# Another order of the transfers ahead of the second feed-forward product, and norm's sum, root and reciprocal at other places

## What is computed

```python
n2 = _rmsnorm(h, g_mlp[i])
h = h + jnp.square(jax.nn.relu(n2 @ w_ff1[i])) @ w_ff2[i]
n3 = _rmsnorm(h, g_ple[i])
h = h + jax.nn.sigmoid(n3 @ w_ple_gate[i]) * (p[i] @ w_ple[i])
```

## Time and profile before

| What | Value |
|---|---|
| Median of the runs | 1781.89 us (1781.26 to 1783.09) |
| The profiled execution, its own time | 1784.99 us |
| Span of its trace | 1782.2 us |
| PE busy | 1689.2 us, 95% of the span |
| DVE, ACT, POOL busy | 966.0, 624.0, 437.5 us |
| Mean DMA rate | 82 GB/s |
| PE, first feed-forward matmuls (line 2172) | about 177 + 175 + 175 us |
| PE, second feed-forward matmuls (line 1827, `wf_hi`, `wf_lo`) | about 159 + 159 + 159 us |

### The profile page before, as it was taken

How to read it: one execution, slowest core, us unless ns; L and a number is a source line. 1 busy time by engine, 2 the same in 40 slices (tenths; PEclk the granted TensorE clock), 3 DMA queues, 4 the chain that set the end, 5 groups by cost and what they waited for, 6 DMA issues and landing times.

```text
span 1782.2 us, 21830 instructions
## 1 busy us (share of the span) xinstructions
PE 1689.2 (95%) x8536; PEld 1325.1 (74%) x8536; DVE 966.0 (54%) x1489; ACT 624.0 (35%) x979; POOL 437.5 (25%) x250
## 2 busy tenths in 40 slices
PE   5899989999899999999999899999979999999997
PEld 4658778787656666668888688888858888888886
DVE  7359999960345566654345644444424444445424
ACT  5332332222355566721234334344412111113323
POOL 2212342222200000212214445445311222222220
PEclk8999999999999999999999999999989999999999
DMA  4202022243200020004432242332352222231112
GB/s 151 80 24 59 25 72 98 68 128 88 60 1 1 2 72 1 1 1 142 161 123 94 74 139 95 105 132 95 142 212 95 95 95 95 95 107 42 42 59 95
DMA packets 101742, 145.38 MB, mean 82 GB/s; under 512 B 17073, under 2 KB 83633, under 8 KB 101649
## 3 DMA queue, kind: packets, MB, share of 16 engines
q1 hardware_dynamic: 97808, 130.45, 22.5%
q10 hardware_dynamic: 3680, 13.63, 2.0%
q0 software_dynamic: 160, 0.02, 0.0%
HBM read 107.51 MB, written 34.73 MB: 80 GB/s over the span
## 4 chain that ended last, share of the span: by engine, by line
PE 86%; DVE 4%; issue 4%; ACT 3%; POOL 2%; DMA 1%; ACTq 0%; SPq 0%; DVEq 0%; POOLq 0%
PE ps L1827 52%; PE ps L2172 14%; PE ps L2057 3%; PE ps L2071 3%; PE ps L2022 2%; PE ps L2041 2%; PE ps L2028 2%; PE ps L1936 2%; PE ps L1884 1%; PE ps L1897 1%; PE ps L2136 1%; DVE prob_a L1558 1%; PE ps L1998 1%; DVE prob_b L1558 1%; PE ps L1855 0%
## 5 line engine op out<-in xcount | busy, mean ns | idle before, releaser
L819 POOL TENSOR_TENSOR w_lo<-w_raw,w_hi 128x1024 fp32r<-128x1024 f32 x67 | 163.0, 2435 | 530.7 <-ACT w_hi L933 530.7
L933 ACT ACTIVATE w_hi<-w_raw 128x1024 fp32r<-128x1024 f32 x67 | 70.8, 1060 | 361.2 <-PE ps L1827 314.7
L1827 PE MATMUL ps<-n_hi,w_hi 128*128 128x512 f32 x576 | 181.4, 397 | 15.8 <-POOL w_lo L819 4.6
L2172 PE MATMUL ps<-b_hi,a_hi 128*128 128x512 f32 x448 | 176.7, 394 | 9.4 <-DVEq L1704 5.8
L1827 PE MATMUL ps<-n_lo,w_hi 128*128 128x512 f32 x576 | 180.4, 395 | 0.0
L1827 PE MATMUL ps<-n_hi,w_lo 128*128 128x512 f32 x576 | 180.0, 394 | 0.0
L1745 DVE TENSOR_TENSOR h<-h,ps 128x2048 f32<-128x2048 f32 x32 | 73.2, 2287 | 189.5 <-PE ps L1827 179.4
L2172 PE MATMUL ps<-b_hi,a_lo 128*128 128x512 f32 x448 | 175.3, 391 | 0.0
L2172 PE MATMUL ps<-b_lo,a_hi 128*128 128x512 f32 x448 | 175.3, 391 | 0.0
L1827 PE MATMUL ps<-hid_hi,wf_hi 128*128 128x512 f32 x512 | 159.2, 392 | 12.8 <-POOL wf_lo L819 12.1
L1442 DVE TENSOR_SCALAR_CACHE_REDUCE tested<-sc,bar_i 128x384 bf16<-128x384 f32 (+2 forms) x192 | 169.0, 943 | 1.7 <-POOL sc L834 0.6
(11 more groups left out here) (304 smaller groups left out, 2917.6 us busy)
## 6 DMA issues: line engine op xcount, KB each, us to landing
f_raw<-in_w_ff_dram SPq DMA_DIRECT2D x32, 512.0 KB, 5.7
hid_scratch<-c_out SPq DMA_DIRECT2D x32, 512.0 KB, 3.5
w_raw<-in_w_ff_dram SPq DMA_DIRECT2D x32, 512.0 KB, 3.6
hid_lo<-hid_scratch SPq DMA_DIRECT2D x32, 512.0 KB, 5.6
w_raw<-in_w_in_dram SPq DMA_DIRECT2D x28, 512.0 KB, 3.7
gates_scratch<-stage ACTq DMA_DIRECT2D x16, 512.0 KB, 2.6
sig_ab<-gates_scratch SPq DMA_DIRECT2D x8, 1024.0 KB, 6.0
x_tok<-in_x_dram SPq DMA_DIRECT2D x8, 512.0 KB, 10.2
```

Source lines behind the costliest of these rows:

```text
L819: pool.tensor_tensor(lo_of(first)[:, :, :], w_raw[s][:, :, :], hi_of(first)[:, :, :].bitcast(F32), ALU.subtract).then_inc(lo_ready, 1)
L933: act.activation(hi_of(first)[:, :, :], w_raw[s][:, :, :], ACT.Copy).then_inc(hi_ready, 1)
L1827: last = pe.matmul(bank(4 * half + 2 * j + t)[0:w, :], wm, xm[:, t * HALF:(t + 1) * HALF], start=(k == 0 and a), stop=(k == total - 1 and ...
L2172: last = pe.matmul(unit_bank(u, PLACE[name]), w[o % 10][:, j, :], x[j][:, b, :], start=name in ("P1", "P2", "P5") and j == 0 and a, stop=j ...
```

## The change

Four edits, all in the feed-forward part. Nothing is computed otherwise, and every engine has as many instructions as before.

- SP: the transfers of weight tiles 2 and 3 of the second matrix go earlier, between hidden and residual tiles; the four quarters of h stand otherwise among the hidden tiles of chunk 1; p comes after weight tiles 4 and 5; and the hidden tiles of chunks 2 to 7 wait in addition until ACT has split all tiles of the chunk before.
- PE: the sum of squares runs behind block product o = 5, not 6.
- ACT and DVE: the root stands at o = 5 ahead of `first_hi(9)` and `first_hi(10)`, not at o = 7 behind `first_hi(12)` and `first_hi(13)`; the reciprocal stands ahead of `add_c22(0)`, not behind it.
- p is turned and split behind chunk 1, not chunk 0.

```diff
@@ SP
             load_hid(0, CHUNK - 1)
+            load_ff2(2)
             store_unit(UNITS_1 - 1)
             sp.wait_ge(a_used, LAST)
             sp.wait_ge(c12_done, UNITS_1)
...
             load_h(0)
+            load_h(1)
+            load_ff2(3)
+            load_h(2)
             for k in range(CHUNK):
                 load_hid(1, k)
-            for q in range(1, 2 * OUT_N):
-                load_h(q)
-            sp.dma_start(p_tok[:, :, :], p2.rearrange("(t q) d -> q t d", q=P)).then_inc(p_loaded, 16)
-            for n in range(2, 4 * FFN):
+            load_h(3)
+            for n in range(4, 4 * FFN):
+                if n == 6:
+                    sp.dma_start(p_tok[:, :, :], p2.rearrange("(t q) d -> q t d", q=P)).then_inc(p_loaded, 16)
                 if n % 4 == 2 and 1 <= n // 4 < FFN - 1:
                     sp.wait_ge(slab_used, FF2_SLAB + 4 * (n // 4))
+                    sp.wait_ge(hid_hi_done, CHUNK * (n // 4 + 1))
                     for k in range(CHUNK):
                         load_hid(n // 4 + 1, k)
                 load_ff2(n)
@@ ACT
                     copy_chain(u, name)
+                if o == 5:
+                    act.wait_ge(sq_summed, 1)
+                    for t in range(2):
+                        act.activation(rms[:, t * HALF:(t + 1) * HALF], bank(4 * t + 3), ACT.Sqrt, bias=eps_c,
+                                       scale=1.0 / D).then_inc(root_done, 1)
                 for ahead_o in HI_AT.get(o, ()) if o < 8 else (o + 6,):
...
                         first_hi(ahead_o)
-                if o == 7:
-                    act.wait_ge(sq_summed, 1)
-                    for t in range(2):
-                        act.activation(rms[:, t * HALF:(t + 1) * HALF], bank(4 * t + 3), ACT.Sqrt, bias=eps_c,
-                                       scale=1.0 / D).then_inc(root_done, 1)
...
-                if i == 0:
+                if i == 1:
                     half = group()
                     act.activation(pt_hi[:, :, :].rearrange("q a n -> q (a n)"), bank(4 * half, 4), ACT.Copy).then_inc(
@@ DVE
             add_c11(1)
+            inverse(2)
             add_c22(0)
-            inverse(2)
             relu(0, 0, first, c11_done)
...
-                if i == 0:
+                if i == 1:
                     half, _, _, _ = at_.group()
                     dve.wait_ge(pt_hi_done, 1)
@@ PE
                 first_product(o, range(0, KT))
-                if o == 6:
+                if o == 5:
                     square_sums((3, 7), SQ3)
...
-                if i == 0:
+                if i == 1:
                     half = group()
                     pe.wait_ge(p_loaded, 16)
```

## The result

| | Before | Changed |
|---|---|---|
| Median of the runs | 1782.41 us (1781.26 to 1783.09, 4 runs) | 1763.93 us (1762.69 to 1764.50, 4 runs) |
| Ratio, 95% interval | | 0.9896 (0.9879 to 0.9913) |
| Span of the trace | 1782.2 us | 1762.7 us |

The changed kernel takes 18.5 us less. The forecast was 20.1 us less (1761.8 us), range 1758.5 to 1767.0. The measured time lies in the range, 2.1 us above the forecast.

The account below looks back on a forecast made before the run. PE, 95% busy, was taken to bound the kernel through its work and two waits: -12.1 - 3.1 - 3.8 - 2.8 + 1.7 = -20.1 us off the median 1781.9 gave 1761.8 us, range 1758.5 to 1767.0.

Parts of the forecast that it names:

- Chunk 0: wait and its low clock: Second product: PE's 12.1 us wait for weight tile 2 and 3.1 us of low clock go, 15.2 us.
- New wait ahead of (0,P3): First product, o = 9: PE stands 2.8 us for add_c22(0), which now stands behind the reciprocal.
- Its low clock: Behind the new wait at o = 9: 1.7 us lost, between 0 and 1.7, at the utmost 2.8.
- Norm part in all: First product: o = 12 starts 3.8 us earlier, 2.8 us of old low clock goes, 1.7 us of new comes.
- o = 12 after o = 4: First product: o = 12 starts at 1005.3 instead of 1009.12, before the 1.7 us of new low clock.
- Turning p behind chunk 1: Second product: 1.91 us of transposes and a short wait move by 43.5 us; costs nothing.
- Bound: PE is 95% busy, so the span is PE's work and waits, the larger at weight tile 2, the smaller at o = 12.
- What is late next: Chunk 0: chunk 1's first hidden tile lands at about 1304.3, add_out(1) ends about 1310.1; 7 us to spare for product 3.
- The added wait on ACT's hidden parts: SP, six chunks: costs SP 2.1 us; first weight tile lands 11.9 us into the chunk, 6 us to spare, nothing lost.
- first rival: First product, o = 9: the clock holds over the new wait, giving 1760.1 us; chance 0.33.
- POOL beside the reciprocal: First product: POOL's lo part for o = 9 runs inside the reciprocal at no cost; otherwise 0.6 us more, 1762.4.
- One step was too short: First product: take_c21(0) ready for o = 12 at 997.0 + 3.3 = 1000.3, before PE needs it at 1005.3.

Follow-up runs that it names:

- the two experiments on each part alone: Against the kernel before: only the transfers and p as changed, 1768.62 us, ratio 0.9922; only sum, root and reciprocal as changed, 1778.75 us, ratio 0.9976.
- the norm part alone: The kernel before with only sum, root and reciprocal as changed, transfers and p as before: 1778.75 us against 1783.22, ratio 0.9976.
- p back: The changed kernel with p turned and split behind chunk 0 as before, its transfer still behind weight tile 5: 1763.76 us, ratio to before 0.9892.
- the kernel with the add first: The changed kernel with the reciprocal behind add_c22(0), as before the change: 1758.83 us, ratio to before 0.9863.
- the kernel with `take_c21(0)` first: The changed kernel with the reciprocal behind add_c22(0), and take_c21(0) directly behind the reciprocal, ahead of three relus and a sum: 1759.42 us, ratio to before 0.9873.
- that with the halves: The changed kernel with the reciprocal in two halves of 512 columns and add_c22(0) between them: 1760.20 us, ratio to before 0.9868.
- tile 2 alone: The kernel before with only weight tile 2 issued early, right behind hidden tile 3 of chunk 0: 1770.31 us against 1782.62, ratio 0.9931.

## Why the prediction was right

| Step, as predicted | Forecast | Measured |
|---|---|---|
| Chunk 0: wait and its low clock | 12.1 + 3.1 = 15.2 us | 15.35 us (product 0 to chunk 2: 104.95 to 89.6) |
| New wait ahead of (0,P3) | 2.8 us | 2.78 us |
| Its low clock | 1.7 us | 1.69 us |
| Norm part in all | 3.8 + 2.8 - 1.7 = 4.9 us | 4.9 us (39.1 to 34.2) |
| o = 12 after o = 4 | 1007.0 - 978.2 = 28.8 us | 28.76 us |
| Turning p behind chunk 1 | 0 | 0 |

The 104.95 us of before are worked out: product 0 starts at 1285.11, chunk 1 at 1346.54, and four products take 43.52 (4 x 10.88, the distance of ACT's two rows at 1357.83 and 1368.71 in the earlier trace rows).

```profile
1285.11 0.61 PE L1827 MATMUL ps<-hid_hi,wf_hi 128*128 128x512 f32 x2
...
1346.54 0.72 PE L1827 MATMUL ps<-hid_hi,wf_hi 128*128 128x512 f32 x2 [0.70 <-DVE h L1745]
```

The 1.69 us: (0,P3) takes 4.41 us, 997.81 to 1002.22, where a block product takes 2.72.

- **Bound.** PE's two waits were set by a place in SP's queue and by one in ACT's program, not by an engine's speed. Both go when the place is changed, each without the other (the two experiments on each part alone).
- **What is late next.** The step on chunk 1's first hidden tile named the right chain (ACT, DVE, `add_out(1)`). By the forecast the tile would land 12.4 us after h was first issued; it took 14.2 (1287.7 to 1301.9). The add ended at 1306.5, and PE needs it 32.6 us after 1280.91, at 1313.5: 7 us to spare, as said.
- **The added wait on ACT's hidden parts.** It was said to bring the first weight tile behind it 1 us later than ACT wants it, and to cost nothing. The row at 1336.61 is that tile: ACT waits 1.04 us longer than for the tile ahead of it (9.91 against 8.87 us of idleness), and PE does not. In later chunks it is more than said, up to 1.87 us, as here in chunk 6, first changed, then before:

```profile
1557.73 1.06 ACT L938 ACTIVATE wf_hi<-w_raw 128x1024 fp32r<-128x1024 f32 x1 [10.74 <-DMA w_raw<-in_w_ff_dram]
```

```profile
1575.43 1.06 ACT L933 ACTIVATE wf_hi<-w_raw 128x1024 fp32r<-128x1024 f32 x1 [8.87 <-PE ps L1827]
```

  This tile lands 8.8 us after its issue at 1548.9, so the 8.0 us that the prediction took as the most were too few. Of the 6 us to spare over 5 are left, and PE's only wait from 1300 us to the end of the product is the 0.63 us ahead of chunk 2.
- **The clock, partly luck.** This was the choice between forecast and first rival. In three executions with this wait (the changed kernel, the norm part alone, p back) its length is 2.78 or 2.79 us, and 1.7 us are lost each time. But the choice was a bet. The three waits of the earlier trace rows stand ahead of every edit, so all ten traces have them, equally long. Behind the one of 2.17 us the clock over 6 us was 0.72 in eight traces and 1.00 in two; behind that of 2.54 or 2.55 us 0.72 in two and 1.00 in eight; behind that of 2.92 us 0.72 in all ten. The first two waits in the kernel with the add first, the other way round than in the earlier trace rows:

```profile
123.10:129.10 6.00, 5.96 (x26) 4.92 (x27) 5.32 (x12) 2.94 (x3) 2.65 (x2) 1.00 0.00 0
329.00:335.00 6.00, 5.94 (x19) 4.74 (x20) 5.68 (x11) 3.11 (x3) 0.00 (x0) 0.72 0.34 132
```

  The prediction also had more rows of this kind than the three that it counted: in the trace before, for one, a wait of 2.57 us at 1764.63 was followed by 0.72, and in the ten traces its like was followed by 0.72 seven times and by 1.00 three times. The Trainium skill ("TensorE: Matmul & The Clock Gate", Part 1) says that the point at which the clock changes varies from run to run; the ten traces agree at three of these waits, and at 2.78 and 2.92 us none of them happened to show it. The longer wait in chunk 0 shows it too: one of 12.14 us was followed by a clock of 0.61 over 8 us before, and one of 12.12 us by 0.72 in the kernel with the norm part alone, 0.8 us apart by the traces.
- **POOL beside the reciprocal.** Three of POOL's subtractions ran inside it in 3.79 us, and it took 6.55 us. No cost, as the row of before had it.
- **One step was too short.** The forecast had (2,P1) ready 3.3 us behind the add, as before behind the reciprocal. There `take_c21(0)` had started 2.4 us behind it (1005.8 to 1008.2) and PE 0.9 us later. Now it starts 5.1 us behind the add (997.7 to 1002.8), so ready would be about 6.0 us, since the three relus, which took 1.89 us before, took 4.62 beside three subtractions of POOL. That is 1003.7, and PE came only at 1007.7, so it cost nothing. With the add first it is the 0.6 us at (2,P1).

**The 2.1 us between forecast and median.** Of these 0.5 us is the kernel before itself: the forecast starts from its median of 1781.9, the result has 1782.4. The rest is the gain. The sum of the parts by the traces is 4.9 + 15.35 = 20.3 us, that of the spans 19.5, that of the medians 18.5. Most of the difference to the spans lies ahead of the change: o = 4 starts at 978.2 in the trace before and at 978.9 in the changed one. The medians have noise of their own: the interval of the ratio is 15.5 to 21.6 us, and 20.3 lies in it. Busy time of the first 72 us, changed kernel, the granted clock being the column ahead of the DMA share:

```profile
0.00:72.00 72.00, 50.87 (x212) 41.39 (x212) 42.07 (x76) 34.16 (x46) 20.40 (x20) 0.88 0.40 123
```

In this stretch the clock was 0.93 in the trace before, 0.88 here and with the add first, 0.98 in the kernel with `take_c21(0)` first, and 0.83 in that with the halves, though the same instructions run there; and o = 4 starts at 977.6 with the highest and 979.9 with the lowest of these. The clock there is not the whole of it: with tile 2 alone it was 0.85, and o = 4 starts at 976.8, earliest of all. So single executions differ by up to 3 us before they reach the change. That this makes up the 1.8 us between parts and medians is possible, not shown.

**A version that beats both** is the changed kernel with the reciprocal behind `add_c22(0)`, as it stood before the change: 1758.83 us, 24 us or 1.4% below the kernel before. The change moved sum, root and reciprocal; moving the first two is worth 8.7 us, moving the reciprocal too takes 3.8 of them back.

## What to carry to other kernels

A wait that ends in a transfer may be a matter of the queue: compare its landing time with that of its like elsewhere (here 18.9 against 3.3 to 8.0 us), and issue it where its buffer comes free instead of where its turn seems to be. When a slow step is moved ahead to shorten one wait, look at the cheap steps it now stands in front of: here 0.69 us of adding behind 6.55 us of reciprocal cost PE 2.8 us and then 1.7 us of clock. Such a wait's price is its length and, in many executions, the low clock behind it, and a wait cut from 2.8 to 1.2 us also saved the latter. Whether the clock falls behind a wait of 2.2 to 2.6 us is not to be read from one trace: the same wait in another execution went the other way.

## What the runs showed of the hardware

- A reciprocal on VectorE took 1.75 us for 256 columns of 128 partitions, 3.35 for 512, 4.95 for 768 and 6.55 for 1024: by these four an estimated 6.25 ns a column and 0.15 us. The last took 6.55 us with one and with three of POOL's subtractions inside it.
- A relu with scale (`SCALAR_TENSOR_TENSOR` on two SBUF operands), 0.63 us each when alone, took 1.5 us each beside POOL's subtractions, and three of these took 4.64 instead of 3.79 us.
- After waits of PE of 5.7 to 5.8 us, three traces lost 2.7 us to the clock of 1.2 GHz (the next two block products took 8.2 us, not 5.4), after 2.8 us three traces lost 1.7, after 1.20 us one lost none. For lengths from 2.1 to 2.6 us the same wait was followed by the low clock in some executions and by full clock in others.
